# A paged latent-attention decode on one core: pages turned by VectorE, scores in 32x32 tiles, a fourth page buffer, and a new order of scores and weighted sums

## The reference

```python
c_past = cache_ckv[page_table].reshape(b_s, past_len, KV_RANK)      # 8 x 2048 x 256
kpe_past = cache_kpe[page_table].reshape(b_s, past_len, HEAD_ROPE)  # 8 x 2048 x 32
# latent_attention, 16 heads, one query a sequence:
s = jnp.einsum('bqhr,bkr->bhqk', q_lat, c) + jnp.einsum('bqhe,bke->bhqk', q_pe, kpe)
s = s.astype(jnp.float32) * scale
p = jax.nn.softmax(jnp.concatenate(scores, axis=-1), axis=-1)
term = jnp.einsum('bhqk,bkr->bqhr', p[..., off:off + nk].astype(c.dtype), c)
```

## Time and profile before

| | |
|---|---|
| median of three runs | 2004.9 us |
| profiled execution | 2008.5 us |
| its span, first to last instruction | 2006.8 us |
| PE, DVE, ACT, POOL busy | 98%, 64%, 41%, 7% |
| mean granted clock of PE | 0.988 of 2.4 GHz |
| decode stage, first scores to end of last scores | 1507.4 to 1575.9 us |

### The profile page before, as it was taken

How to read it: one execution, slowest core, us unless ns; L and a number is a source line. 1 busy time by engine, 2 the same in 40 slices (tenths; PEclk the granted TensorE clock), 3 DMA queues, 4 the chain that set the end, 5 groups by cost and what they waited for, 6 DMA issues and landing times.

```text
span 2006.8 us, 41571 instructions
## 1 busy us (share of the span) xinstructions
PE 1965.1 (98%) x17584; PEld 1878.2 (94%) x17584; DVE 1280.1 (64%) x1781; ACT 820.4 (41%) x1243; POOL 132.3 (7%) x231
## 2 busy tenths in 40 slices
PE   8999999998999999999999999999989999999998
PEld 7999999988999999999999999997656899999998
DVE  6445486697469577576875856655764349668474
ACT  5332233343245244355452534554654244345252
POOL 3002002010000000000000000000048000000000
PEclk9999999989999999999999999998999999999999
DMA  7233234864342322234322322231248422323222
GB/s 150 85 102 88 77 91 115 278 134 97 95 137 85 124 87 98 72 105 116 97 87 83 126 89 87 78 101 51 53 119 234 151 70 79 127 85 125 86 74 75
DMA packets 260625, 211.49 MB, mean 105 GB/s; under 512 B 42372, under 2 KB 235426, under 8 KB 260450
## 3 DMA queue, kind: packets, MB, share of 16 engines
q1 hardware_dynamic: 248528, 187.52, 31.6%
q0 software_dynamic: 6656, 13.69, 2.4%
q10 hardware_dynamic: 5266, 7.78, 1.2%
HBM read 195.22 MB, written 10.33 MB: 102 GB/s over the span
## 4 chain that ended last, share of the span: by engine, by line
PE 68%; DVE 3%; ACT 2%; issue 2%; SPq 1%; DMA 0%; DVEq 0%; ACTq 0%
PE ps L2459 25%; PE ps L2487 25%; PE ps L2388 6%; PE ps L2401 2%; PE ps L3034 1%; PE ps L2941 1%; PE ps L3190 1%; PE ps L3067 1%; SPq L637 1%; PE ps L3011 1%; PE ps L2835 1%; SPq L652 1%; DVE wl L1666 0%; DVE xl L1617 0%; DVE mx L2210 0%
## 5 line engine op out<-in xcount | busy, mean ns | idle before, releaser
L2388 PE MATMUL ps<-xh,wh 128*128 128x260 f32 x1088 | 286.9, 285 | 2.6 <-DVE xl L1617 1.4
L2388 PE MATMUL ps<-xl,wh 128*128 128x260 f32 x1088 | 283.7, 283 | 0.0
L2487 PE MATMUL ps<-xoh,wh 128*128 128x260 f32 x992 | 281.3, 284 | 1.3 <-DVE sq L1833 1.3
L2487 PE MATMUL ps<-xoh,wl 128*128 128x260 f32 x992 | 281.0, 283 | 0.0
L2487 PE MATMUL ps<-xol,wh 128*128 128x260 f32 x992 | 280.6, 283 | 0.0
L2459 PE MATMUL ps<-xh,wh 128*128 128x260 f32 x872 | 228.8, 284 | 0.6 <-DVE wl L1666 0.6
L1065 ACT ACTIVATE wh<-rw 128x1024 fp32r<-128x1024 f32 (+1 forms) x135 | 138.8, 1029 | 218.6 <-PE ps L2459 151.7
L2459 PE MATMUL ps<-xl,wh 128*128 128x260 f32 x872 | 227.0, 282 | 0.0
L2388 PE MATMUL ps<-xh,wl 128*128 128x260 f32 x1088 | 219.3, 283 | 0.0
L988 ACT ACTIVATE wh<-raw 128x1024 fp32r<-128x1024 f32 (+1 forms) x90 | 100.5, 1116 | 283.0 <-PE ps L2388 251.2
L2388 PEld LDWEIGHTS ps<-xh,wh 128*128 128x128 f32 x1088 | 205.6, 189 | 6.9 <-issue 3.9
(11 more groups left out here) (550 smaller groups left out, 4214.9 us busy)
## 6 DMA issues: line engine op xcount, KB each, us to landing
rw<-ffn_w_gate SPq DMA_DIRECT2D x33, 1024.0 KB, 5.3
rw<-ffn_w_up SPq DMA_DIRECT2D x33, 1024.0 KB, 7.9
rw<-ffn_w_down SPq DMA_DIRECT2D x12, 2048.0 KB, 7.7
raw<-ffn_w_gate SPq DMA_DIRECT2D x22, 512.0 KB, 3.8
raw<-ffn_w_up SPq DMA_DIRECT2D x22, 512.0 KB, 3.7
raw<-ffn_w_down SPq DMA_DIRECT2D x16, 704.0 KB, 4.8
rw<-ffn_w_down SPq DMA_DIRECT2D x6, 1536.0 KB, 6.6
cb<-cache_ckv SPq DMA_DIRECT2D x72, 128.0 KB, 3.9
```

What stands on the lines that cost most here:

```text
L2388: got = mm(ps[0:width, bank + half, 0:HALF], w[par_][:, k * width:k * width + width], src[:, k0 + k, half * HALF:half * HALF + HALF], star ...
L2487: got = mm(ps[:, bank + mat, T0], w[:, cols], src[:, j, k, :], start=first and k == 0 and m == 0 and s == 0, stop=k == 3 and m == 1, skip_ ...
```

## The change

- **Turned pages.** DVE's 32x32 block transpose replaces PE's turns and the copies out of PSUM: `turned(b, 0)` for the keys (128x512), `turned(b, 1)` to `turned(b, 4)` for 64 features of the latents each (128x1024), from SBUF to SBUF. Each 32x32 block stays on its 32 partitions, so partition group a holds the pages with number a modulo 4, and every group holds all 32 features of a chunk.
- **Scores.** `past_scores(b, c)`: products in tiles of 32 rows and 32 columns, 16 for the keys (c = 0) and 32 for each c from 1 to 4. Row group a writes PSUM bank a, column group j its 32 partitions. Banks 0 to 3 hold the scores of one sequence alone, so the next one's wait for `d_e`. The queries must lie on every row group: `qrep`, made by one DMA to memory and eight back, issued by POOL.
- **Layout of pages.** A page comes to 32 partitions, four tokens on each, 4 KB of latents and 512 bytes of keys. The exponential writes the probabilities in the order that this asks for.
- **Loads.** SP issues 8 pages of latents and 4 of keys one by one; POOL issues the other 8 and 12 as two and three gathers by index, 128 rows each (`indirect_dma_start`), with row numbers that it works out once. There is a fourth latent buffer `cbw` in the place of `wh` and `wl`: sequence 2 waits for the last use of those in the attention, sequence 3 for its end, b from 4 on for the weighted sums of b-4.
- **Order on PE.** Wait for exp(b), turn the probabilities, `past_scores(b+1, 0)` and `(b+1, 1)`, weighted sums of b, `past_scores(b+1, 2)` to `(b+1, 4)`. ACT, not DVE, copies the turned probabilities. The output half that stood behind the last scores comes behind the last probabilities' turns and weighted sums.
- **Around it.** All four early output tiles have wide buffers `w4a`, `w4b` (split by `wide_hi` on ACT, `wide_lo` on DVE) in the places of `cb0`, `kb0` and `cb1`; `uv` takes the place of `cbT` and is loaded after all scores; two splits leave the attention loop (`if i in (0, 2)` for `if i % 2 == 0`).

The core of the diff:

```diff
-SP_PG = 9
-N_SP, N_POOL = 2 * SP_PG - 1, 2 * (NPG - SP_PG) + 1
+SP_PG, SP_KEYS = 8, 4
+CB, KB_BUFS = 4, 3
 AHEAD = 5
...
                 kb2 = be0[:, :, :].rearrange("p k m -> p (k m)")[:, 0:NPG * DR].rearrange("p (g e) -> p g e", g=NPG)
-                cb, kb = [cb0, cb1, cb2], [kb0, kb1, kb2]
+                cb, kb = [cb0, cb1, cbw, cb2], [kb0, kb1, kb2]
         ps = ctx.enter_context(nc.psum_tensor("ps", [P, 8, 512], F32))
...
 
-        uv = cb[2][:, :, :].rearrange("p g r -> p (g r)")[:, 0:RT * NH * DV].rearrange("p (t m) -> p t m", t=RT)
+        uv = cbT[:, :, :, :].rearrange("p c q k -> p (c q k)")[:, 0:RT * NH * DV].rearrange("p (t m) -> p t m", t=RT)
+        page_of = qrep1[:, 0, 0, :]
+
+        def wide(d):
+
+            part = (w4a, w4b)[d // 2]
+            return part[:, d % 2, 0, :], part[:, d % 2, 1, :]
...
+        qrep0 = cst[:, C_COS:C_COS + NQ * NB * HP].rearrange("p (s b h) -> p s b h", s=NQ, b=NB)
+        qrep = (qrep0, qrep1[:, :, :, :])
+        qpe = rbc[:, 0:NB * HP].rearrange("p (b h) -> p b h", b=NB)
+        dr_q = nc.dram_tensor("dec_q_rows", (P, RT, NB * HP), F32).ap()
         of = sq[:, 0, 0:NH // 2 * NB].rearrange("p (i b) -> p i b", b=NB)
         olat = sq[:, 1, 0:RT * NB * NH].rearrange("p (r b h) -> p r b h", r=RT, b=NB)
...
+        def page(buf, g):
+
+            a = HP * (g % NQ)
+            return buf[a:a + HP, ROWS * (g // NQ):ROWS * (g // NQ + 1), :].rearrange("p v r -> p (v r)")
+
+        def latents_free(eng, b):
+
+            if b == 0:
+                eng.wait_ge(a_qs[0], 64 * (NH // 4))
+                eng.wait_ge(a_qs[1], 64 * (NH // 4))
+            elif b == 1:
+                eng.wait_ge(a_ve, NH // 2)
+            elif b == 2:
+                eng.wait_ge(w_used, PR0 + NH // 4)
+            elif b == 3:
+                eng.wait_ge(a_ol, NH // 2)
+            else:
+                eng.wait_ge(d_o, b - CB + 1)
+
+        def keys_free(eng, b):
+
+            if b >= KB_BUFS:
+                eng.wait_ge(d_t, (NCT + 1) * (b - KB_BUFS) + 1)
...
+            def keys(b):
+
+                keys_free(sp, b)
+                for g in range(SP_KEYS):
+                    sp.dma_start(page(kb[b % KB_BUFS], g), inp["cache_kpe"][bass.ds(numbers[b][g], 1)].rearrange(
+                        "a (u v) r -> (a u) (v r)", v=ROWS)).then_inc(d_key[b % KB_BUFS], 16)
+
+            def pages(b):
+
+                latents_free(sp, b)
+                for g in range(SP_PG):
+                    sp.dma_start(page(cb[b % CB], g), inp["cache_ckv"][bass.ds(numbers[b][g], 1)].rearrange(
+                        "a (u v) r -> (a u) (v r)", v=ROWS)).then_inc(d_in[b % CB], 16)
+
+            sp.wait_ge(d_pt, 16)
             sp.wait_ge(q_ev, NQT)
             nope_rows(0)
...
+            for b in range(NB):
+                pages(b)
+                if b == 0:
+                    keys(0)
+                if b == 1:
+                    for m in range(AHEAD, NB):
+                        number(m)
+                if b + 1 < NB:
+                    keys(b + 1)
+            for d in range(2, 4):
+                load(WO0 + d, (WO0 + d) % 2, wo[:, :, d * P:d * P + P], KD)
+            sp.wait_ge(d_s, (NCT + 1) * NB)
             sp.dma_start(uv[:, :, :], uvd).then_inc(d_uv, 16)
...
+                    dve.wait_ge(d_gkey[b % KB_BUFS], (b // KB_BUFS + 1) * 16 * (NQ - SP_KEYS // NQ))
+                elif c == 1:
+                    dve.wait_ge(d_in[b % CB], IN_1 + (b // CB + 1) * 16 * SP_PG)
+                    dve.wait_ge(d_gin[b % CB], (b // CB + 1) * 16 * (NQ - SP_PG // NQ))
                 if b >= 1:
-                    dve.wait_ge(d_s, b)
-                copy(cbT[:, q // 4, (q % 4) * 512:(q % 4) * 512 + 512], ps[:, (0, 1, 7)[(b * 9 + q) % 3], :]).then_inc(d_td, 1)
+                    dve.wait_ge(d_s, (NCT + 1) * (b - 1) + c + 1)
+                if c == 0:
+                    V.transpose(kbT, kb[b % KB_BUFS].rearrange("p g e -> p (g e)")).then_inc(d_t, 1)
+                else:
+                    V.transpose(cbT[:, c - 1, :, :].rearrange("p q (g u) -> p g q u", u=HP),
+                                cb[b % CB][:, :, 2 * HP * (c - 1):2 * HP * c].rearrange("p g (q r) -> p g q r", q=2)).then_inc(d_t, 1)
 
...
             for b in range(NB):
-                dve.wait_ge(d_s, b + 1)
-                own(V.tensor_reduce(mb[:, b:b + 1], ps[:, 2 + b % 2, :], AX.X, ALU.max))
+                if b + 1 < NB:
+                    turned(b + 1, 0)
+                dve.wait_ge(d_s, (NCT + 1) * (b + 1))
+                own(V.tensor_reduce(mb[:, b:b + 1], ps[:, 0:NQ, 0:P], AX.XY, ALU.max))
                 ts(nmb[:, b:b + 1], mb[:, b:b + 1], -SCALE, None, ALU.mult).then_inc(d_m, 1)
                 if b + 1 < NB:
-                    turned(b + 1, 1)
-                    turned(b + 1, 3)
-                else:
-                    wide_lo(0)
-                dve.wait_ge(d_pt2, b + 1)
-                if b >= 1:
-                    dve.wait_ge(d_o, b)
-                copy(pbT[:, :, :], ps[:, 4, :].rearrange("p (m q) -> p m q", m=NQ)).then_inc(d_pe, 1)
-                if b + 1 < NB:
-                    turned(b + 1, 5)
-                    turned(b + 1, 7)
+                    for c in range(1, NCT + 1):
...
+            def wide_hi(d):
+
+                act.wait_ge(d_o, NB - 3 + d // 2)
+                act.wait_ge(w_in[(WO0 + d) % 2], slots.arrived(WO0 + d))
+                run(wide(d)[0], raw[(WO0 + d) % 2][:, 0:KD * P], ACT.Copy).then_inc(w_hi, 1)
+
+            def latents(b):
+
+                act.wait_ge(d_o, b + 1)
+                run(ob[:, b, :], ps[:, 5 + b % 2, 0:R], ACT.Copy).then_inc(d_oe, 1)
 
             for b in range(NB):
-                if b + 1 < NB:
-                    turned(b + 1, 0)
-                else:
-                    act.wait_ge(d_o, NB - 1)
-                    for j in range(2):
-                        act.wait_ge(w_in[(WO0 + j) % 2], slots.arrived(WO0 + 2 + j))
-                        run(w4h[:, j, :], raw[(WO0 + j) % 2][:, 0:KD * P], ACT.Copy).then_inc(w_hi, 1)
-
                 act.wait_ge(d_m, b + 1)
                 if b >= 1:
                     act.wait_ge(d_pt2, b)
-                run(pb, ps[:, 2 + b % 2, :], ACT.Exp, bias=nmb[:, b:b + 1], scale=SCALE, accum_out=lb[:, b:b + 1]).then_inc(d_e, 1)
-                if b + 1 < NB:
-                    for q in range(2, 9, 2):
-                        turned(b + 1, q)
-                act.wait_ge(d_o, b + 1)
-                run(ob[:, b, :], ps[:, 5 + b % 2, 0:R], ACT.Copy).then_inc(d_oe, 1)
+                run(pb.rearrange("p (v a u) -> p a v u", v=ROWS, a=NQ), ps[:, 0:NQ, 0:P].rearrange("p a (v u) -> p a v u", v=ROWS),
+                    ACT.Exp, bias=nmb[:, b:b + 1], scale=SCALE, accum_out=lb[:, b:b + 1]).then_inc(d_e, 1)
+                if b >= 1:
+                    latents(b - 1)
+                act.wait_ge(d_pt2, b + 1)
+                run(pbT[:, :, :], ps[:, 4, :].rearrange("p (m q) -> p m q", m=NQ), ACT.Copy).then_inc(d_pe, 1)
...
+            def past_scores(b, c):
+
+                if b == 0 and c == 0:
+                    pe.wait_ge(d_qr, 16 * (1 + 2 * NQ))
+                if b >= 1 and c == 0:
+                    pe.wait_ge(d_e, b)
+                pe.wait_ge(d_t, (NCT + 1) * b + c + 1)
+                for q in range(2 if c else 1):
+                    n = 2 * (c - 1) + q
+                    for a in range(NQ):
+                        rows = slice(HP * a, HP * a + HP)
+                        w, keys_ = (qrep[n // NQ][rows, n % NQ, b, :], cbT[rows, c - 1, q, :]) if c else (qpe[rows, b, :], kbT[rows, :])
+                        for j in range(NQ):
+                            got = mm(ps[HP * j:HP * j + HP, a, 0:P], w, keys_[:, P * j:P * j + P],
+                                     start=c == 0, stop=c == NCT and q == 1, skip_group_check=True)
+                got.then_inc(d_s, 1)
+
+            for c in range(NCT + 1):
+                past_scores(0, c)
 
             for b in range(NB):
-                j = b % 2
-
-                pe.wait_ge(d_ta, 5 * (b + 1))
...
                 pe.wait_ge(d_e, b + 1)
                 if b >= 1:
                     pe.wait_ge(d_pe, b)
@@ -3222,13 +3219,12 @@
                     got = turn(ps[:, 4, m * P:m * P + P], pb[:, m * P:m * P + P])
                 got.then_inc(d_pt2, 1)
                 if b + 1 < NB:
-                    for q in range(4, 9):
-                        turned(b + 1, q)
...
@@ -3236,16 +3232,19 @@
                     pe.wait_ge(a_ol, NH // 2)
                 for m in range(NQ):
                     for c in range(NQ):
-                        got = mm(ps[HP * c:HP * c + HP, 5 + j, 0:R], pbT[:, m, HP * c:HP * c + HP], cb[b % 3][:, 4 * c + m, :],
+                        got = mm(ps[HP * c:HP * c + HP, 5 + b % 2, 0:R], pbT[:, m, HP * c:HP * c + HP], cb[b % CB][:, NQ * c + m, :],
                                  start=m == 0, stop=m == NQ - 1, skip_group_check=True)
 ```

(42 more changed lines are left out.)

247 lines of the change are left out of this document (91 added, 156 removed).

## The result

The median went from 2005.9 us to **2038.8 us** (2036.2 to 2041.5), a ratio of 1.0163, 95% interval 1.0143 to 1.0182: 33 us slower, where 17 us faster was forecast and 2009 was the upper end of the range. The profiled execution has a span of 2039.7 us.

A forecast was written before the change was run, and what follows sets the result against it. PE, busy 98% of the span, was taken as the bound. Sequences at 7.0 us against 9.37 put last scores 19.3 us earlier; +1.9 for the last exp gives -17.4: 1988 us, range 1983 to 2009.

The forecast's parts named there:

- the last exponential: End of decode stage: output products that filled PE beside exp come behind the wait, 1.9 us lost once.
- the start: Start of decode stage: first scores end at 1507.6, before the change at 1510.2.
- the period of a sequence: Decode stage: 7.0 us a sequence against 9.37, from DVE's cycle of 7.0 and PE's of 6.6.
- Turns off PE: Decode stage: 36 PE turns, 4.42 us a sequence, go; DVE's four latent transposes cost 1.27 us each, 5.1 in all.
- Exposed exponential: Decode stage: nothing on PE is left beside exp, 1.85 us of idle PE in every sequence.
- Pace of the small products: Decode scores in 32x32 tiles: 7.3 ns an instruction, 2.1 us a sequence; bounds 6.4 and 25.5 ns.
- changes of shape: Decode stage on PE: each change of tile shape costs about 0.13 us, three inside a sequence, 0.4 us.
- Sixteen tiles of 102 ns would allow 6.4: Decode scores: lower bound of the pace, 6.4 ns an instruction, 1.8 us a sequence.
- the first rival: Decode stage: clock falls at times or pace is 13 ns; 7.6 to 8.8 us a sequence, 1992 to 2000; chance 0.26.
- each two instructions: 288. This is the price that decides.: Decode scores: 144 products a sequence, two instructions each, priced by array pace at 2.1 us a sequence.
- Loads: Decode page loads: hidden with some 4 us margin, cost nothing; gathers taken at 1 to 1.3 us, hidden up to 1.8.
- The rule cited against the change: Decode scores: a floor of about 25 ns start to start makes a sequence 11.7 us, 2025; chance 0.03.

The follow-up runs named there:

- bidle: Kernel before, with the four page turns beside the exponential moved behind it, so PE waits there with no instruction more; 2023.7 us against 2004.3.
- fill_noload: Changed kernel with weighted sums behind all next score parts, three dummy 512-column products a sequence, no page loads from sequence 4 on; 2020.3 us.
- n64: Changed kernel with score products of 64 keys instead of 128 in parts 2 to 4, the same number of instructions; 2033.1 us.
- warm: Changed kernel with two extra unused 512-column products on PE ahead of each wait for the exponential; 2041.7 us.
- spread: Changed kernel with the 16 weighted sums of a sequence issued in four groups between the next sequence's score parts; 2040.4 us.
- fill: Changed kernel with weighted sums behind all next score parts and three dummy 512-column products a sequence, page loads kept; 2034.1 us.
- cut64: Kernel before, with its 512-key latent score products cut into pieces of 64 keys, 232 matmuls a sequence; 2013.6 us against 2006.6.
- after: The changed kernel itself, with nothing further edited, against the kernel before; 2038.8 us, ratio 1.0163.
- noload: Changed kernel without page loads from sequence 4 on (keys from 3 on), computing on old pages; 2025.5 us.
- cut: Kernel before, with its 512-key latent score products cut into pieces of 32 keys, 360 matmuls a sequence; 2058.6 us against 2004.3.

## Why the prediction was wrong

**By its own steps**, from the last one back. Forecast: last scores at 1556.6, +1.9, 2008.5 - 17.4. Measured: first scores end at 1510.2 (forecast 1507.6), then 7 x 13.75, last scores at 1606.4. Last scores are 30.5 us behind those of before, and 1.9 us for the last exponential make 32.4 of the 33 us. Against the forecast they are 49.8 us late: 2.6 from the start, and 47.2 from the period of a sequence, 13.7 instead of 7.0.

- *Turns off PE: right.* The transposes are 1.21 us each (forecast 1.27), 0.68 for the keys; two lines of VectorE's groups:

```profile
L2269 DVE STREAM_TRANSPOSE cbT<-cb 128x1024 f32<-128x1024 f32 x20 | 23.1, 1213 | 0.3 <-issue 0.3
L2267 DVE STREAM_TRANSPOSE tb<-kb 128x512 f32<-128x512 f32 x4 | 2.7, 680 | 0.0
```

- *Exposed exponential: right in size* (1.78 to 2.01 us, 1.86 on average, against 1.85), and by bidle in its price, as long as nothing else slows the stage.
- *Pace of the small products: the term that was mis-sized.* Forecast 7.3 ns, 2.1 us a sequence with 0.4 for changes of shape. Measured at 2.4 GHz (fill_noload, to the next start): 0.31 for the keys, 1.10 for part 1, 1.25, 0.99 and 1.00 for parts 2 to 4: 4.65 us, 10 to 20 ns each with the changes of shape, 13 within a long run. The row chosen had 8 columns, these have 128, and n64 shows that columns count in part. "Sixteen tiles of 102 ns would allow 6.4" took for granted that sixteen run at once; at 13 ns about eight would, by the same estimate of 102 ns for each. With the measured pace PE needs 7.1 + 1.8 = 8.9 us a sequence, and the same sum gives last scores at 1507.6 + 7 x 8.9 = 1569.9, -6.0 + 1.9, a median of 2001: inside the range, just past the first rival.
- *The step that failed: "each two instructions: 288. This is the price that decides."* It gave each instruction a time in the array and none to its coming. 120 matmuls a sequence became 324, and one block in 9.4 us became 2.6 in what should have been 7 or 8.9. That is a block per 2.7 to 3.4 us; the tightest stretches of any run show one per 3.3 to 4, and about 5 while pages are loaded. 2.6 x 5 = 13 us is about what the stage took. Of the 34 us that seven sequences took beyond 8.9 each, 16 are the gaps themselves; the other 18, by subtraction, are PE's work in stretches at the lower clock. Since warm, spread and fill moved the clock between 0.61 and 0.87 and the time by less than 5 us, the supply of instructions is what holds the whole. Why a block takes 5 us beside page loads was not found. No rival had this step.
- *Clock: it fell as the first rival said, but it isn't the price.* It was 0.72 in the stage. Among wide products the exposed exponential leaves 1.00 (bidle), and gaps of up to 1.3 us leave 1.00 (cut64). Among the small ones it fell behind the exponential's wait alone, twice in after and again in noload, and behind gaps of 2.5 to 5 us, also in cut. Raising it gave no time (warm, fill). The rival's 7.6 to 8.8 us a sequence was far from 13.7 all the same.
- *Loads: hidden from PE's waits, as forecast* (no releaser on PE is a page), POOL's gathers 0.95 us each against a bound of 1.8. But they cost 13 us (noload), which the prediction put at nothing. Without them the gaps fell from 16.7 to 9.9 us and the clock rose from 0.72 to 0.79. The profile lists the instruction queue among the queues of the same 16 DMA engines; how the two get in each other's way was not tried further.
- *The rule cited against the change* ("TensorE: Matmul & The Clock Gate", Part 1, of the Trainium skill: no less than 25 ns from start to start) was rightly doubted: 13 ns within a run here, 8.6 in cut. Its 2025 is nearer to 2038.8 than the forecast, but by luck: at 2.4 GHz no run of products went as slowly as 25 ns. At 1.2 GHz some did, as the 64 products from 1574.83 on (2.01 us, 28 ns each), which the forecast's clock of 1.00 had left out.
